# Expert products of a mixture-of-experts layer: split weights as moving operand, or unsplit 128x128 weight tiles as stationary operand

## The chip, the cores and the metric

One NeuronCore of a Trainium2 chip runs the whole program. The metric is the device time of one execution in microseconds (us). All data are float32.

## The reference, cut to what matters

One diffusion step of a one-layer hybrid model: 640 tokens (512 latent, 128 context) of 1024 features pass an mLSTM and an S5 branch and then an expert-choice mixture of experts. The change touches that last part alone:

```python
def ec_moe(h, w_router, b_router, w1, w3, w2):          # 16 experts, D 1024, FF 1536
    aff = jax.nn.softmax((h @ w_router) + b_router, axis=-1)
    topv, topi = lax.top_k(jnp.swapaxes(aff, 1, 2), cap) # 64 of 512 latents, 16 of 128 context tokens
    xe = h[topi]                                         # 80 rows of 1024 for each expert
    hid = silu(xe @ w1[e]) * (xe @ w3[e])                # 80 x 1536
    ye = (hid @ w2[e]) * topv                            # 80 x 1024
    return zeros.at[topi].add(ye)                        # scatter-add over tokens
```

Each expert reads three matrices of 1024x1536 float32, 18.9 MB; all sixteen read 302 MB.

## The kernel before, in words

The program is a row of blocks, each with a program for SP (which issues the weight loads), POOL (GpSimd, which issues gathers and scatters), PE (TensorE), ACT (ScalarE) and DVE (VectorE). First come the modulation, the S5 branch and the mLSTM heads; then the gates and projections (matmuls of L1309); then the router (from L1412), which turns the normalised tokens to rows, writes them to DRAM (`h2`) and picks 80 tokens for each expert; then the experts (from L1497); then a last block that reads the summed rows back and applies the final norm (from L1790).

Ahead of the expert block `load_piece` (L1242 to L1246) loads the first pieces: six while the last projections run, three more once the `h2` rows are written.

The expert block before. Each expert's hidden width of 1536 is cut into FG = 6 groups of 256. A piece is 1 MB: the 1024x256 columns of `w1` or `w3`, or 256 rows of `w2`, in a ring of three places for each name. Each piece is split for a product in three parts: ACT writes the high part `p_h` in the fp32r format (`high`, L1704), DVE writes `p_l`, the weight less that (`low`, L1749). The gathered tokens are turned by PE (`begin`, L1631) and split in the same way (L1698, L1741). In `up` (L1673) the 128x80 token tile is the stationary operand and 256 weight columns move, three matmuls for each of the 8 feature tiles: high by high, high by low, low by high. ACT applies silu (L1712), DVE multiplies (L1767), PE turns the hidden rows (`turn`, L1656), ACT and DVE split them (L1717, L1771), and `down` (L1646) multiplies them with `w2`, 512 columns moving. `take_y` (L1758, L1759) scales the 80x1024 result by the gate value; POOL clears a flag (L1608) and adds the rows into DRAM with an indirect DMA (L1610). Gathers (L1599) run two experts ahead. The order of PE in a step is up w1, turn, up w3, down of the step before. Loops (`Fori`) run over pairs of experts. SP waits for `w1_split`, `w3_split` and `w2_split`, which DVE raises when it has split a piece, before it loads into its place.

Other lines that the prediction reads: L676 multiplies 128x128 float32 stationary tiles by 80 float32 columns (S5 additions); L196 does it by 2 columns, L989 by 128 columns; L668 and L1441 are PE transposes of 128x128.

Of the kernel before, what the change touches and what calls it, by code (L numbers as in the profile page):

```python
# [20 lines left out]
P = 128  # L21
# [18 lines left out]
FG = 6  # L40
NRAW = 3
FT = FF // P // FG
# [29 lines left out]
def program(nc, ar, out):  # L72
    with ExitStack() as ctx:
# [1168 lines left out]
        PLACE = {"w1": (2, 7, 4), "w3": (3, 8, 0), "w2": (6, 5, 1)}  # L1242
        def load_piece(sp, name, e, q):
            sp.dma_start(place[:, PLACE[name][q % NRAW]],
                         ar["w_e" + name[1]][bass.ds(e, 1), q].rearrange("e p n -> p (e n)")
                         ).then_inc(sem(f"{name}_in{q % NRAW}"), 16)  # L1246

        with ExitStack() as st:
# [29 lines left out]
            @block.sync  # L1279
            def _(sp):  # L1280
                sp.dma_start(wr[:].rearrange("p k e -> p (k e)"), ar["w_router"]).then_inc(sem("wr_in"), 16)
                load_weights(sp, len(plan))

                sp.wait_ge(sem("parts_ready"), ends["B3"])
                load_piece(sp, "w1", 0, 0)
                load_piece(sp, "w3", 0, 0)
                load_piece(sp, "w2", 0, 0)
                load_piece(sp, "w1", 0, 1)
                load_piece(sp, "w3", 0, 1)
                sp.wait_ge(sem("parts_ready"), ends["O0"])  # L1290
                load_piece(sp, "w2", 0, 1)
# [110 lines left out]
        gidx = sb("gidx", [CAP, E], I32, moe)  # L1402
        with ExitStack() as st:  # L1403
# [9 lines left out]
            def token_rows(t):  # L1413

                return place[:, (0, 0, 1, 1, 4)[t], (t % 2) * D:(t % 2 + 1) * D]

            @block.sync
            def _(sp):
                sp.wait_ge(sem("h2_out"), 16 * NT)
                load_piece(sp, "w1", 0, 2)  # L1420
                load_piece(sp, "w3", 0, 2)
                load_piece(sp, "w2", 0, 2)
# [75 lines left out]
        with ExitStack() as st:  # L1498
# [4 lines left out]
            HC, HF = FT * CAP, FT * P  # L1503
            sl, hid = (rows[0:CAP, (4 + x) * D - x * D // 2:(4 + x) * D - x * D // 2 + D // 2].rearrange("p (b n) -> p b n", b=2)
                       for x in range(2))

            flag = sb("flag", [1, 1], F32, st)  # L1510
            x_h = sb("x_h", [P, 2, KD, CAP], F32R, st)
            x_l = sb("x_l", [P, 2, KD, CAP], F32R, st)
            hid_h = sb("hid_h", [P, 2, HC], F32R, st)
            hid_l = sb("hid_l", [P, 2, HC], F32R, st)
            PR = 4
            p_h = sb("p_h", [P, PR, KD * HF], F32R, st)
            p_l = sb("p_l", [P, PR, KD * HF], F32R, st)

            def parts(o, q, name):

                r = (3 * (o + q) + {"w1": 0, "w3": 1, "w2": 5}[name]) % PR
                return p_h[:, r, :], p_l[:, r, :]

            def up_tiles(ap):
                return ap.rearrange("p (k f) -> p k f", k=KD)

            def down_tiles(ap):
                return ap.rearrange("p (t d) -> p t d", t=FT)

            def raw(q, name):  # L1530
                return place[:, PLACE[name][q % NRAW], :]

            block = st.enter_context(nc.Block())

            def known(i, o, q, least):

                return not isinstance(i, int) or 2 * FG * i + o + q >= least

            def landed_at(i, o, q):

                return 16 * (2 * FG // NRAW) * i + 16 * ((o + q) // NRAW + 1)

            def experts(eng, begin, step, after=0):

                def half(i, o, h, coming=None):
                    for x, q in enumerate(range(h * FG // 2, (h + 1) * FG // 2)):
                        if coming and x == after:  # L1550
                            begin(*coming)
                        step(i, o, q)

                if after:
                    step(0, 0, 0)
                begin(0, 0)
                for q in range(1 if after else 0, FG // 2):
                    step(0, 0, q)
                half(0, 0, 1, (0, 1))
                half(0, FG, 0)  # L1560
                with eng.Fori(1, E // 2) as i:
                    half(i, -FG, 1, (i, 0))
                    half(i, 0, 0)
                    half(i, 0, 1, (i, 1))
                    half(i, FG, 0)
                half(E // 2 - 1, FG, 1)

            @block.sync
            def _(sp):
                def pieces(e, q):  # L1570

                    sp.wait_ge(sem("w1_split"), FG * e + (q - NRAW + 1))
                    load_piece(sp, "w1", e, q)
                    sp.wait_ge(sem("w3_split"), FG * e + (q - NRAW + 1))
                    load_piece(sp, "w3", e, q)
                    sp.wait_ge(sem("w2_split"), FG * e + (q - NRAW))
                    if q:
                        load_piece(sp, "w2", e, q - 1)
                    else:
                        load_piece(sp, "w2", e - 1, FG - 1)  # L1580

                sp.wait_ge(sem("w1_split"), 1)
                load_piece(sp, "w1", 0, 3)
                sp.wait_ge(sem("w3_split"), 1)
                load_piece(sp, "w3", 0, 3)
                for q in (4, 5):
                    pieces(0, q)
                with sp.Fori(1, E) as e:
                    for q in range(FG):
                        pieces(e, q)  # L1590
                sp.wait_ge(sem("w2_split"), FG * E - NRAW)
                load_piece(sp, "w2", E - 1, FG - 1)

            @block.gpsimd
            def _(pool):
# [7 lines left out]
                def scatter(e):  # L1603
# [11 lines left out]
                gather(0)  # L1615
                gather(1)
                for e in range(E):
                    if e + 2 < E:
                        gather(e + 2)
                    scatter(e)  # L1620
# [3 lines left out]
            PARTS = ((0, 0), (0, 1), (1, 0))  # L1624

            @block.tensor
            def _(pe):
                def begin(i, u):
                    pe.wait_ge(sem(f"xe_in{u}"), 16 * i + 16)
                    for k in range(KD):  # L1630
                        mm = pe.transpose(PS[4 + k // 4][:, (k % 4) * CAP:(k % 4 + 1) * CAP],  # L1631
                                          xe[:, u, k * P:(k + 1) * P], ident[0:CAP, 0:CAP])
                    mm.then_inc(sem("x_turned"), 1)

                def down(i, o, q):

                    n = 2 * FG * i + (o + q)
                    if q == 0 and known(i, o, q, FG):
                        pe.wait_ge(sem("y_ready"), 2 * i + o // FG)
                    pe.wait_ge(sem("hid_split"), n + 1)  # L1640
                    pe.wait_ge(sem("w2_split"), n + 1)
                    w2p = [down_tiles(x) for x in parts(o, q, "w2")]
                    for t in range(FT):
                        for x in range(2):
                            for j, (a, b) in enumerate(PARTS):
                                mm = pe.matmul(PS[2 + x][0:CAP, :], (hid_h, hid_l)[a][:, q % 2, t * CAP:(t + 1) * CAP],  # L1646
                                               w2p[b][:, t, x * 512:(x + 1) * 512],
                                               start=(q == 0 and t == 0 and j == 0),
                                               stop=(q == FG - 1 and t == FT - 1 and j == 2))
                    mm.then_inc(sem("down_done"), 1)  # L1650

                def turn(i, o, q):

                    pe.wait_ge(sem("hid_ready"), 2 * FG * i + (o + q + 1))
                    for t in range(FT):
                        mm = pe.transpose(PS[6 + q % 2][:, t * CAP:(t + 1) * CAP], hid[:, q % 2, t * P:(t + 1) * P],  # L1656
                                          ident[0:CAP, 0:CAP])
                    mm.then_inc(sem("hid_turned"), 1)

                def step(i, o, q):  # L1660
                    n = 2 * FG * i + (o + q)
                    u = (o // FG) % 2
                    if q == 0:
                        pe.wait_ge(sem("x_split"), 2 * i + (o // FG + 1))
                    if known(i, o, q, 2):
                        pe.wait_ge(sem("hid_ready"), n - 1)
# [13 lines left out]
                    elif known(i, o, q, 1):  # L1680
                        turn(i, o - FG, FG - 1)
# [241 lines left out]
```

## Time and profile before

| what | us |
|---|---|
| median of three runs (2022.3 to 2042.13) | 2038.01 |
| the profiled execution, its own time | 2040.35 |
| its span in the trace | 2038.3 |

### The profile page before, as it was taken

How to read it: one execution, taken by the hardware profiler on the slowest of the kernel's cores; microseconds unless marked ns; L12 is line 12 of the kernel's file. 1: busy time of each engine (PE TensorE's matmuls, PEld its weight loads, DVE VectorE, ACT ScalarE, POOL GpSimd, SP SyncE). 2: the span in 40 equal slices, each digit the busy share in tenths (PEclk: the TensorE clock that was granted, in tenths of full speed). 3: DMA queues.
4: the chain of work that ended last, by engine and by line, in shares of the span. 5: the costliest groups of instructions: out<-in, count | busy, mean ns of one | idle time of the engine just before them, and what ended most of it. 6: DMA issues, size and time to landing. Idle time of an engine off the chain costs nothing. (4 is left out here: it accounts for less than half of the span.)

```text
span 2038.3 us, 26524 instructions
## 1 busy us (share of the span) xinstructions
PE 1787.2 (88%) x10568; PEld 1407.4 (69%) x10568; DVE 1241.2 (61%) x1689; ACT 940.3 (46%) x1207; POOL 132.8 (7%) x92
## 2 busy tenths in 40 slices
PE   4775557999898986999997499999999999999993
PEld 2464444555464645999995488888888888888882
DVE  4577761013131314555554788888888888888874
ACT  3342222021212122444434377766666777766651
POOL 2600000000000000000000011100000011111000
PEclk8887768999898977999998699999999999999996
DMA  9032324102020110111230799999999999999953
GB/s 379 27 119 94 93 93 155 41 0 93 11 93 11 60 75 12 73 52 53 83 124 3 253 348 387 376 379 379 371 378 377 376 377 374 378 374 377 365 187 109
DMA packets 66698, 403.15 MB, mean 198 GB/s; under 512 B 12084, under 2 KB 18740, under 8 KB 25284
## 3 DMA queue, kind: packets, MB, share of 16 engines
q1 hardware_dynamic: 61476, 384.36, 49.7%
q0 software_dynamic: 5152, 17.84, 3.1%
q8 instruction: 47, 0.77, 0.2%
q14 instruction: 23, 0.19, 0.0%
HBM read 383.47 MB, written 16.56 MB: 196 GB/s over the span
## 5 line engine op out<-in xcount | busy, mean ns | idle before, releaser
L1749 DVE TENSOR_TENSOR p_l<-place,p_h 128x2048 fp32r<-128x2048 f32 x288 | 650.4, 2286 | 97.8 <-ACT p_h L1704 97.8
L1704 ACT ACTIVATE p_h<-place 128x2048 fp32r<-128x2048 f32 x288 | 540.3, 1911 | 26.3 <-PEq L1403 20.9
L1673 PE MATMUL bank<-p_h,x_h 128*80 128x256 f32 x1536 | 434.0, 283 | 1.8 <-DVE x_l L1741 1.8
L1673 PE MATMUL bank<-p_l,x_h 128*80 128x256 f32 x1536 | 429.6, 280 | 0.0
L1673 PE MATMUL bank<-p_h,x_l 128*80 128x256 f32 x1536 | 428.1, 279 | 0.0
L1673 PEld LDWEIGHTS bank<-p_h,x_h 128*80 128x80 f32 x1536 | 227.8, 148 | 9.4 <-DVE x_l L1741 2.0
L1673 PEld LDWEIGHTS bank<-p_l,x_h 128*80 128x80 f32 x1536 | 228.0, 148 | 6.1
L1673 PEld LDWEIGHTS bank<-p_h,x_l 128*80 128x80 f32 x1536 | 227.9, 148 | 0.0
L1309 PE MATMUL bank<-a_h,w_h 128*128 128x320 f32 x576 | 183.7, 319 | 19.6 <-DVE w_l L1390 10.9
L1309 PE MATMUL bank<-a_l,w_h 128*128 128x320 f32 x576 | 180.8, 314 | 0.0
L1309 PE MATMUL bank<-a_h,w_l 128*128 128x320 f32 x576 | 180.5, 313 | 0.0
L1646 PE MATMUL bank<-p_h,hid_h 128*80 128x512 f32 x384 | 150.6, 392 | 1.9 <-DVE hid_l L1771 1.9
L1646 PE MATMUL bank<-p_h,hid_l 128*80 128x512 f32 x384 | 151.8, 395 | 0.0
L1646 PE MATMUL bank<-p_l,hid_h 128*80 128x512 f32 x384 | 150.3, 391 | 0.0
L1717 ACT ACTIVATE hid_h<-bank 128x160 fp32r<-128x160 f32 x96 | 29.2, 304 | 241.1 <-PE bank L1656 241.1
L1000 PE MATMUL bank<-place,hT 128*128 128x512 f32 x320 | 138.0, 592 | 0.0
L1309 PEld LDWEIGHTS bank<-a_h,w_h 128*128 128x128 f32 x576 | 110.4, 192 | 26.3 <-DVE w_l L1390 12.7
L985 PE MATMUL bank<-hT,place 128*128 128x512 f32 x256 | 110.6, 592 | 2.2 <-PEq L866 2.2
L1000 PEld LDWEIGHTS bank<-place,hT 128*128 128x128 f32 x320 | 60.7, 190 | 74.8 <-issue 74.6
L1309 PEld LDWEIGHTS bank<-a_l,w_h 128*128 128x128 f32 x576 | 110.8, 192 | 0.0
L1309 PEld LDWEIGHTS bank<-a_h,w_l 128*128 128x128 f32 x576 | 110.7, 192 | 0.0
L1204 DVE TENSOR_TENSOR nd<-bank,rsb 128x257 f32<-128x257 f32 x32 | 13.6, 426 | 126.9 <-ACT rsb L1143 126.5
(353 smaller groups left out, 2304.2 us busy)
## 6 DMA issues: line engine op xcount, KB each, us to landing
place<-w_e_dram SPq DMA_DIRECT2D x288, 1024.0 KB, 7.6
place<-w_ada_dram SPq DMA_DIRECT2D x12, 2048.0 KB, 7.8
place<-w_qk_dram SPq DMA_DIRECT2D x4, 2048.0 KB, 9.2
place<-w_vo_dram SPq DMA_DIRECT2D x4, 2048.0 KB, 11.2
place<-w_gate_dram SPq DMA_DIRECT2D x4, 2048.0 KB, 7.4
place<-w_pAB_dram SPq DMA_DIRECT2D x4, 1536.0 KB, 6.4
place<-w_out_dram SPq DMA_DIRECT2D x2, 2048.0 KB, 7.3
xT<-xT_dram SPq DMA_DIRECT2D x1, 2560.0 KB, 17.7
```

The costliest lines, as they stand in the source:

```text
L985: mm = pe.matmul(PS[u % 2][:, :], w, hT[:, k, 0:LAT], start=(k == 0), stop=(k == 7))
L1000: mm = pe.matmul(PS[u % 2][:, :], hT[:, k, t * P:(t + 1) * P], wslot(c)[:, k, :], start=(k == 0), stop=(k == 7))
L1204: dve.tensor_tensor(nd[:, d, :], PS[3 + d][:, 0:DH + 1], Qs[:, d, :], ALU.add).then_inc(sem("nd_ready"), 1)
L1309: mm = pe.matmul(PS[bank][:, 0:TH], wp[:, n % RING, j * P:(j + 1) * P], ap[:, n % RING, x * TH:(x + 1) * TH], start=(k == 0 and i == 0), s ...
L1646: mm = pe.matmul(PS[2 + x][0:CAP, :], (hid_h, hid_l)[a][:, q % 2, t * CAP:(t + 1) * CAP], w2p[b][:, t, x * 512:(x + 1) * 512], start=(q == ...
L1673: mm = pe.matmul(PS[q % 2][0:CAP, at:at + HF], (x_h, x_l)[a][:, u, k, :], wp[b][:, k, :], start=(k == 0 and j == 0), stop=(k == 7 and j == 2))
L1704: act.activation(parts(o, q, name)[0], raw(q, name), ACT.Copy).then_inc(sem(f"{name}_high"), 1)
L1717: act.activation(hid_h[:, q % 2, :], PS[6 + q % 2][:, 0:HC], ACT.Copy).then_inc(sem("hid_high"), 1)
L1749: dve.tensor_tensor(l, raw(q, name), h.bitcast(F32), ALU.subtract).then_inc(sem(f"{name}_split"), 1)
```

## The change

- The weights of the experts are no longer split. In `up` a 128x128 tile of `w1` or `w3` is the stationary operand and the 80 tokens of `x` (features on partitions) move; the output is the hidden layer with its features on partitions, 12 tiles of 80 columns in two PSUM banks for each matrix. `down` uses 128x128 tiles of `w2` as stationary operand and `hid` moves. All of these are plain float32.
- Output y comes out turned; ACT copies it to SBUF (`take_y`), PE turns it back (`turn_y`, eight 128x80 tiles for each expert), DVE scales it (`leave_y`), POOL adds it to DRAM. The turning of the hidden rows, the splits of tokens and hidden values and the flag go.
- The pieces are 1.5 MB each, 4 for each matrix, 12 for each expert, 192 in all, in one ring of ten slots: five in the old place, five in a new tile `ring_tail`. PE raises `piece_used` after the last matmul on a piece, and SP waits for that. Five pieces are loaded while the projections end, three at the start of the router block, two once the `h2` rows are written. The token rows of the router stand in the last two slots of the new ring.
- Gathers are issued three experts ahead. The loops over experts are unrolled.
- PE's order for expert e: the four pieces of w1 (after the first `turn_y(e-2)`, after the third `turn_x(e+1)`), the four of w3, then `down(e-1)`.

The core of the diff:

```diff
-FG = 6
-FT = FF // P // FG
+NF = FF // P
+NR, PIECE, AHEAD_MOE = 10, 3072, 10
...
+        def load_piece(sp, n):
+            name, e, c = moe_pieces[n]
+            sp.dma_start(ring(n), ar["w_e" + name[1]][e, c]).then_inc(sem(f"piece_in{n % NR}"), 16)
...
-                    pool.memset(flag[:], 0.0).then_inc(sem("ys_free"), 1)
-                    pool.wait_ge(sem("ys_free"), e + 1)
...
+                for n in range(AHEAD_MOE, len(moe_pieces)):
+                    sp.wait_ge(sem("piece_used"), n - NR + 1)
+                    load_piece(sp, n)
...
-                        for k in range(KD):
-                            for j, (a, b) in enumerate(PARTS):
-                                mm = pe.matmul(PS[q % 2][0:CAP, at:at + HF], (x_h, x_l)[a][:, u, k, :], wp[b][:, k, :],
-                                               start=(k == 0 and j == 0), stop=(k == 7 and j == 2))
...
+                def turn_y(e):
+
+                    pe.wait_ge(sem("yT_ready"), e + 1)
+                    if e:
+                        pe.wait_ge(sem("y_ready"), e)
+                    for d in range(KD):
+                        mm = pe.transpose(PS[6 + d // 4][0:CAP, (d % 4) * P:(d % 4 + 1) * P], yT[:, d, :], ident)
+                    mm.then_inc(sem("y_turned"), 1)
+
+                def up(name, e, bank):
+                    for c in range(4):
+                        n = piece_at[name, e, c]
+                        have_piece(n)
+                        w = ring(n)[:, 0:2 * FF].rearrange("p (k f) -> p k f", k=2)
+                        for k in range(2):
+                            for f in range(NF):
+                                mm = pe.matmul(PS[bank + f // 6][:, (f % 6) * CAP:(f % 6 + 1) * CAP],
+                                               w[:, k, f * P:(f + 1) * P], x[:, e % 2, 2 * c + k, :],
+                                               start=(c == 0 and k == 0 and f % 6 == 0), stop=(c == 3 and k == 1),
+                                               skip_group_check=True)
+                        mm.then_inc(sem("piece_used"), 1)
+                        if name == "w1" and c == 0 and e >= 2:
+                            turn_y(e - 2)
+                        if name == "w1" and c == 2 and e + 1 < E:
+                            turn_x(e + 1)
...
+                        w = ring(n)[:, 0:3 * D].rearrange("p (t d) -> p t d", t=3)
+                        for t in range(3):
+                            for d in range(KD):
+                                mm = pe.matmul(PS[4 + d // 4][:, (d % 4) * CAP:(d % 4 + 1) * CAP],
+                                               w[:, t, d * P:(d + 1) * P], hid[:, e % 2, 3 * c + t, :],
+                                               start=(c == 0 and t == 0 and d % 4 == 0), stop=(c == 3 and t == 2),
+                                               skip_group_check=True)
...
+                for e in range(E):
+                    pe.wait_ge(sem("x_ready"), e + 1)
+                    if e:
+                        pe.wait_ge(sem("silu_ready"), e)
+                    up("w1", e, 0)
+                    if e:
+                        pe.wait_ge(sem("hid_ready"), e)
+                    up("w3", e, 2)
+                    if e:
+                        down(e - 1)
+                down(E - 1)
+                turn_y(E - 1)
...
-                    act.activation(parts(o, q, name)[0], raw(q, name), ACT.Copy).then_inc(sem(f"{name}_high"), 1)
...
-                    dve.tensor_tensor(l, raw(q, name), h.bitcast(F32), ALU.subtract).then_inc(sem(f"{name}_split"), 1)
```

## Rows read from the trace of the kernel before

**Rows 1.** The page: DMA busy tenths and GB/s in 40 equal slices.

```profile
DMA  9032324102020110111230799999999999999953
GB/s 379 27 119 94 93 93 155 41 0 93 11 93 11 60 75 12 73 52 53 83 124 3 253 348 387 376 379 379 371 378 377 376 377 374 378 374 377 365 187 109
```

**Rows 2.** Stretches: PE, PEld, DVE, ACT, POOL busy (x records), PEclk, DMA share, GB/s.

```profile
1149.50:1157.00 7.50, 5.65 (x28) 5.41 (x29) 5.02 (x4) 2.56 (x3) 0.94 (x1) 0.50 0.87 294
...
1160.00:1950.00 790.00, 789.12 (x5784) 694.65 (x5783) 697.10 (x518) 557.77 (x488) 77.49 (x43) 1.00 0.99 373
```

**Rows 3.** SP's DMA queue waiting between 1200 and 1900 us: us, times, longest.

```profile
SPq L1244 <- DVE p_l L1749: 577.7, 242, 4.4
```

**Rows 4.** PE's timeline in the expert block: x transposes, fp32r matmuls 21 starts apart.

```profile
1149.57 1.33 PE L1631 MATMUL bank<-consts,hT 80*128 80x80 f32 x8 [5.31 <-DMA hT<-h_dram,gidx]
...
1281.26 0.72 PE L1631 MATMUL bank<-consts,hT 80*128 80x80 f32 x8
...
1973.68 0.28 PE L1673 MATMUL bank<-p_h,x_h 128*80 128x256 f32 x1
...
1976.13 0.28 PE L1673 MATMUL bank<-p_h,x_h 128*80 128x256 f32 x1
```

**Rows 5.** Timeline of the end of the expert block, and the end of its last loads.

```profile
1930.08 30.81 SPq L1244 DMA_DIRECT2D place<-w_e_dram  x10
...
1988.12 0.74 DVE L1759 TENSOR_SCALAR hT<-bank,gval 80x512 f32<-80x512 f32 x1
...
1989.29 1.42 POOL L1610 DMA_INDIRECT moe_dram<-hT,gidx  x1 [0.28 <-POOL flag L1608]
```

**Rows 6.** PE's timeline: start us, us, stationary (128*128, 128*16), then moving operand, records.

```profile
565.80 7.31 PE L989 MATMUL bank<-hT,place 128*128 128x128 f32 x64
...
119.02 7.16 PE L697 MATMUL bank<-CA,bbz 128*16 128x128 f32 x64
...
242.38 3.70 PE L676 MATMUL bank<-U,place 128*128 128x80 f32 x32
...
248.65 1.05 PE L196 MATMUL bank<-sel,adar 128*128 128x2 f32 x8 [0.72 <-ACT adar L202]
```

**Rows 7.** Durations of single records of these lines (ns, min/median/max).

```profile
L989 PE MATMUL bank<-hT,place x256: 272/275/276, 372.6 to 685.6; 128*128 128x128 f32 x128
...
L676 PE MATMUL bank<-U,place x128: 235/275/422, 114.8 to 245.8; 128*128 128x80 f32 x128
...
L196 PE MATMUL bank<-sel,adar x96: 251/251/374, 14.4 to 310.6; 128*128 128x2 f32 x96
```

**Rows 8.** Timeline of PE in the router (128x128 transposes), then of SP, POOL and ACT.

```profile
1117.15 1.97 PE L1441 MATMUL bank<-consts,hT 128*128 128x128 f32 x16
...
1129.12 27.06 SPq L1244 DMA_DIRECT2D place<-w_e_dram  x6
...
1145.53 0.97 POOL L1599 DMA_INDIRECT hT<-h_dram,gidx  x1 [20.80 <-POOLq L1403]
...
1150.94 0.77 ACT L1698 ACTIVATE x_h<-bank 128x320 fp32r<-128x320 f32 x2 [2.40 <-PE bank L1631]
```

**Rows 9.** The costliest groups of ACT and DVE: busy us, mean ns, idle before.

```profile
L1749 DVE TENSOR_TENSOR p_l<-place,p_h 128x2048 fp32r<-128x2048 f32 x288 | 650.4, 2286 | 97.8 <-ACT p_h L1704 97.8
L1704 ACT ACTIVATE p_h<-place 128x2048 fp32r<-128x2048 f32 x288 | 540.3, 1911 | 26.3 <-PEq L1403 20.9
```

**Rows 10.** Two stretches of L676, and the unrolled projections (columns of rows 2).

```profile
137.90:139.90 2.00, 2.00 (x11) 2.00 (x11) 1.97 (x3) 0.60 (x1) 0.00 (x0) 0.50 0.04 8
139.90:142.40 2.50, 2.50 (x24) 2.49 (x23) 2.43 (x3) 0.00 (x0) 0.00 (x0) 1.00 0.00 0
...
242.40:246.00 3.60, 3.60 (x34) 3.53 (x32) 3.53 (x4) 0.63 (x2) 0.00 (x0) 1.00 0.00 0
...
870.00:1090.00 220.00, 210.20 (x1368) 203.85 (x1367) 116.78 (x205) 92.77 (x172) 0.00 (x0) 0.98 0.19 72
```

**Rows 11.** DMA of instructions between 870 and 1090 us: packets, MB, share.

```profile
q8 instruction: 11, 0.18, 0.3%
```

More of the change, by code:

```diff
@@ L1284, in _ @@
                 sp.wait_ge(sem("parts_ready"), ends["B3"])
[L1285 to L1289, printed above, removed]
+                for n in range(3):
+                    load_piece(sp, n)
                 sp.wait_ge(sem("parts_ready"), ends["O0"])
-                load_piece(sp, "w2", 0, 1)
+                load_piece(sp, 3)
+                sp.wait_ge(sem("parts_ready"), ends["O1"])
+                load_piece(sp, 4)
             @block.tensor
@@ L1530, in raw @@
-            def raw(q, name):
-                return place[:, PLACE[name][q % NRAW], :]
-            block = st.enter_context(nc.Block())
[L1537 to L1566, printed above, removed]
+            x = sb("x", [P, 2, KD, CAP], F32, st)
@@ L1582, in _ @@
[L1582 to L1592, printed above, removed]
+                for n in range(AHEAD_MOE, len(moe_pieces)):
+                    sp.wait_ge(sem("piece_used"), n - NR + 1)
+                    load_piece(sp, n)
@@ L1613, in scatter @@
                                             ).then_inc(sem(f"y_out{e % 2}"), 16)
-                gather(0)
-                gather(1)
+                for e in range(3):
+                    gather(e)
                 for e in range(E):
-                    if e + 2 < E:
-                        gather(e + 2)
+                    if e + 3 < E:
+                        gather(e + 3)
                     scatter(e)
@@ L1630, in begin @@
                     for k in range(KD):
-                        mm = pe.transpose(PS[4 + k // 4][:, (k % 4) * CAP:(k % 4 + 1) * CAP],
-                                          xe[:, u, k * P:(k + 1) * P], ident[0:CAP, 0:CAP])
+                        mm = pe.transpose(PS[6 + k // 4][:, (k % 4) * CAP:(k % 4 + 1) * CAP],
+                                          xe[:, e % 2, k * P:(k + 1) * P], ident[0:CAP, 0:CAP])
                     mm.then_inc(sem("x_turned"), 1)
[L1635 to L1644, printed above, removed]
-                            for j, (a, b) in enumerate(PARTS):
[L1646 to L1650, printed above, removed]
@@ new lines, in down @@
+                def down(e):
+                    pe.wait_ge(sem("hid_ready"), e + 1)
+                    if e:
+                        pe.wait_ge(sem("yT_ready"), e)
+                    for c in range(4):
+                        n = piece_at["w2", e, c]
+                        have_piece(n)
+                        w = ring(n)[:, 0:3 * D].rearrange("p (t d) -> p t d", t=3)
[5 more added lines that the diff above has]
+                                               skip_group_check=True)
+                        mm.then_inc(sem("piece_used"), 1)
+                        if e == E - 1 and c == 0:
+                            turn_y(e - 1)
@@ L1732, in _, with take_x @@
-                experts(act, begin, step, after=1)
-                finish(E // 2 - 1, FG, FG - 1)
+                def take_x(e):
+                    act.wait_ge(sem("x_turned"), e + 1)
+                    if e >= 2:
+                        act.wait_ge(sem("piece_used"), piece_at["w3", e - 2, 3] + 1)
+                    for y in range(2):
+                        ins = act.activation(x[:, e % 2, 4 * y:4 * y + 4, :].rearrange("p k c -> p (k c)"),
+                                             PS[6 + y][:, 0:4 * CAP], ACT.Copy)
+                    ins.then_inc(sem("x_ready"), 1)
@@ new lines, in take_y @@
+                def take_y(e):
+                    act.wait_ge(sem("piece_used"), piece_at["w2", e, 3] + 1)
+                    if e:
+                        act.wait_ge(sem("y_turned"), e)
+                    for y in range(2):
+                        ins = act.activation(yT[:, 4 * y:4 * y + 4, :].rearrange("p k c -> p (k c)"),
+                                             PS[4 + y][:, 0:4 * CAP], ACT.Copy)
+                    ins.then_inc(sem("yT_ready"), 1)
+                take_x(0)
+                for e in range(E):
+                    if e + 1 < E:
+                        take_x(e + 1)
+                    act.wait_ge(sem("piece_used"), piece_at["w1", e, 3] + 1)
+                    if e:
+                        act.wait_ge(sem("hid_ready"), e)
+                    for h in range(2):
+                        ins = act.activation(sl[:, h, :], PS[h][:, 0:6 * CAP], ACT.Silu)
+                    ins.then_inc(sem("silu_ready"), 1)
+                    if e:
+                        take_y(e - 1)
@@ new lines, in _ @@
+                for e in range(E):
+                    if e >= 2:
+                        leave_y(e - 2)
+                    dve.wait_ge(sem("silu_ready"), e + 1)
+                    dve.wait_ge(sem("piece_used"), piece_at["w3", e, 3] + 1)
+                    if e >= 2:
+                        dve.wait_ge(sem("piece_used"), piece_at["w2", e - 2, 3] + 1)
+                    for h in range(2):
+                        ins = dve.tensor_tensor(hid[:, e % 2, 6 * h:6 * h + 6, :].rearrange("p f c -> p (f c)"),
+                                                sl[:, h, :], PS[2 + h][:, 0:6 * CAP], ALU.mult)
+                    ins.then_inc(sem("hid_ready"), 1)
```

193 lines of the change are left out of this document (46 added, 147 removed).

## The prediction

> **What bounds the kernel now.** I read the page first, for the stages. Its 40 slices are 51 us each. From slice 24 to 38 the DMA row stands at 9 and the GB/s row between 348 and 387: these are the experts. Between the first slice and slice 21 no more than 155 GB/s are moved [rows 1]. The reader should see that nothing ahead of about 1100 us is touched by the change, so it is the expert block that has to be priced. I read next the stretches of that block. From 1160 to 1950 us PE is busy 789.12 of 790 us and the 16 DMA engines have a share of 0.99 at 373 GB/s, both at once, at full clock [rows 2]. Then SP's waits: its queue stands 577.7 us, in 242 waits, for DVE to have split a piece [rows 3], so loads start when a place is free, and places come free at the pace of the split chain.
>
> So two limits lie almost on each other. The weights: 16 x 3 x 1024 x 1536 x 4 bytes are 302 MB, and 302 MB at the 377 GB/s of the best slices takes 801 us. The matmuls: an fp32r matmul of 256 columns follows the one before at 2.45 us / 21 = 117 ns [rows 4], and PE does 3 x 16 x 96 = 4608 of these, and 1152 of 512 columns; their end is near 1987 us, only some 26 us after the last load's landing at 1960.9 us [rows 5]. A change gains only if it relieves both; it loses as soon as either one grows. This one leaves the bytes as they are.
>
> **The change, part by part.**
>
> *Products of the experts.* Each expert needs 8 x 12 tiles for w1, as many for w3, and 12 x 8 for w2: 288 products of a 128x128 stationary tile with 80 moving columns, 4608 in all. A plain float32 product is two LDWEIGHTS and two MATMULs, so 9216 pairs of records. What does one pair cost? The trace of before has exactly this shape at L676. Its fourth stretch lies at full clock and takes 3.70 us for 32 records: (3.70 - 0.235) / 31 = 111.8 ns from start to start (a record at full clock lasts 0.235 us [rows 7]). L989 has the same stationary tile and 128 moving columns: (7.31 - 0.275) / 63 = 111.7 ns. L196 has it with 2 moving columns: (1.05 - 0.251) / 7 = 114 ns [rows 6, 7]. Two, eighty or 128 moving columns cost the same. What sets the pace is therefore the load of the 128 stationary columns and not what streams, and the 80 tokens' short stream buys nothing. I take 111.7 ns: 9216 x 0.1117 = 1029.4 us. The nearest rows bound it: L697 loads only 16 stationary columns for 128 moving ones, (7.16 - 0.27) / 63 = 109.4 ns, a record's 0.27 us as in L989 [rows 6], which I take as the low end for any pair of this kind that doesn't hide its load; and 117 ns if the expert block with its full DMA traffic slowed it to the fp32r pace [rows 4]. That is 1008 to 1078 us.
>
> [...]
>
> *Transposes.* Tokens: 8 for each expert, as before, (0.72 - 0.235) / 7 = 69 ns apart at full clock [rows 4], a record's 0.235 us as at L676: 128 x 0.070 = 8.9 us. Output: 8 for each expert are new, 128 moving columns each; L1441 does 16 in 1.97 us, (1.97 - 0.27) / 15 = 113 ns [rows 8], 128 x 0.113 = 14.5 us. The 192 transposes of hidden rows go. PE's whole work is then 1029.4 + 8.9 + 14.5 = 1052.8 us, 65.8 us for each expert, where before an expert took 52 us, (1987 - 1152.7) / 16.
>
> *What goes from ACT and DVE.* The 288 high parts and 288 low parts, 540 and 650 us of busy time [rows 9]. They lie beside PE and DMA. Their going is worth nothing by itself once PE is the bound: DVE keeps two scalings and two products for each expert, ACT a handful of copies.
>
> *The ring.* A piece of 1.573 MB lasts PE 24 products x 2 x 0.1117 = 5.36 us, and DMA at 377 GB/s 4.17 us. Ten pieces are ahead at the start and SP refills faster than PE uses, so PE never waits for a piece, and the DMA share falls to about 302 MB / 1055 us = 286 GB/s, some 77%. So I cost the loading at nothing; PE's work on the pieces hides it, and were that cover gone, DMA's 801 us would still be the smaller of the two limits.
>
> *Waits on PE.* `turn_y(e-2)` needs two ACT copies of 128x320 (0.43 us each by [rows 8]: 0.77 us for two); it stands behind one piece, 5.4 us. `turn_x(e+1)` needs the two scalings of DVE (0.74 us each [rows 5]); it stands two pieces, 10.7 us, behind `turn_y`. silu and the product for expert e are needed only after four pieces of w2, 21 us. The gather of expert e+3 is queued on POOL ahead of the scatter of expert e, waits for `turn_x(e+1)`, and has more than one expert, 65 us, until it is used. What stands behind these waits on PE is everything, so a miss would count in full, but the shortest cover is seven times what it covers. I cost them at nothing, with 0 to 1 us for each expert (0 to 16 us) kept for the range.
>
> *Start.* The first gather is issued at 1145.53 us and PE turns the tokens from 1149.57 us [rows 4, 8]. The two extra pieces are issued once `h2` is written, at 1129.12 us before [rows 8], and 3.1 MB take 8 us, so the gather finds the queues free as before. ACT's copies end at 1151.7 us; the low part's split of tokens falls out, and the first product starts at 1151.8 instead of 1152.7 us. PEclk is 0.50, the level of 1.2 GHz, until 1157 us, and 1.00 from 1160 us on [rows 2]; 5.3 us at half rate lose 2.7 us.
>
> *End.* After the last product: two copies of ACT and two hops 1.1 us, then the transposes (counted), then two scalings 1.5 us. Before, L1759 ends at 1988.86 us and from there to the end of the span are 49.4 us; the scatter's issue is at 1989.29 us, 0.43 us behind it [rows 5], and without the flag I save 0.3 us of these.
>
> **Sum.** 1151.8 + 1052.8 + 2.7 + 1.1 + 1.6 = 2210.0; + 49.4 - 0.3 = 2259.1 us of span. The profiled execution took 2.05 us more than its span and lies 2.3 us above the median of the runs, so the two cancel: 2259 us, a change of +221 us, 11% slower.
>
> **The rivals.**
>
> *A, faster: the load hides and the weights' transfer is the bound.* Place: the spacing of the 9216 pairs. If loads of the next tile ran wholly beside the stream of 80 columns, a pair would cost what the stream takes; from 5.36 us a piece it decides from the point where a piece costs PE less than 4.17 us, or a pair less than 87 ns. Then the 182 pieces not loaded ahead take 759 us from about 1157 us on, the last is used and turned by about 1924 us, and the end is at 1975 us. For it speaks that the moving operand is now only 80 columns and that the split work of two engines is gone. Against it speak three lines of rows 6 with 2, 80 and 128 columns at one pace. Chance 6%. [...]
>
> *B, the clock stays or falls to 1.2 GHz.* PE streams fewer columns in a given time than before. At half clock pairs are some 214 ns apart, twice as far as at full clock: in L676's second stretch 2.0 us at 0.50 hold 11 records, the next 2.5 us at 1.00 hold 24 [rows 10]; a block wholly at this level costs 2 x 1052.8 us, and the end is near 3310 us. Against it: the same L676 pace was under way at 137.9 us at 0.50 and the clock rose to 1.00 during it, and at 242.4 us it was at 1.00 all through [rows 10]. Those stretches are short. Chance 4%.
>
> *C, the unrolled program starves PE of instructions.* Between 870 and 1090 us, also unrolled, 2735 records of PE came with 11 packets of instructions [rows 10, 11], one for some 250. The new block has 18,900 PE records, so about 76 packets, and DMA is at 77% share and not at 19% as there. If PE stood 2 us for each packet (an estimate: half of the 4.0 us from the first gather's issue to PE's start [rows 4, 8]), it is 152 us more: 2411 us. Against it: PE is busy 210 of 220 us in that unrolled stage. Chance 6%; a part of it, 20 to 40 us, is more likely than the whole.
>
> *D, the pipeline of small waits costs over 16 us*, for instance because PE stands for the two copies, the two scalings and the hops between, some 3 us [rows 5, 8], once for each expert: 16 x 3 us = 48 us, 2307 us. Chance 3%.
>
> **How the numbers follow.** The forecast 81%, A 6%, B 4%, C 6%, D 3%. The range from the bounds: low 2259 - 21 = 2238, and 6 us less for the start, 2232; high 2259 + 49 (117 ns) and a few us of waits, 2315, which takes in D. Left out are A, B and the dear half of C. A measurement of this kernel tells about 1% from no change: faster by over 1% is A, 6%; within 1% 1%; slower 93%.
>
> **What would show it.** L1673's successors should stand 111 to 112 ns apart in the timeline at PEclk 1.00, 24 x 2 in 5.4 us, PE busy over 99% from 1160 to 2200 us, PEld nearer to PE than before; the DMA share of that stretch near 0.77 and under 300 GB/s; SP's queue waiting for PE (`piece_used`) most of its time; DVE and ACT busy under 10% there. PE waiting for a DMA, or PE starts under 90 ns apart, would make the forecast wrong at its root (A); PEclk under 1.00 would be B; idle time of PE put down to issue would be C.

## The result and the profile after

The changed kernel takes 2360.03 us (median of four runs, 2349.64 to 2363.95) against 2039.74 us: ratio 1.158, 95% interval 1.151 to 1.166, slower. The sign was forecast, the size was not: 2259 us had been given, with a range up to 2315. The span of its profiled execution is 2358.7 us. An execution of any of these programs takes one of two courses through the mLSTM stage, and PE begins to turn the first expert's tokens at 1147 to 1152 us in the late one and at 1132 to 1137 us in the early one; the profiled executions of the kernels before and after took the late one.

The page of the changed kernel, with the rows that answer to [rows 1] and the one of PE's granted clock:

```profile
span 2358.7 us, 30959 instructions
...
PE   4965579989898699998599999999999999999993
...
DVE  4577720122121455564300000000000000000003
ACT  3333210222212244444000000000000000000001
POOL 1500000000000000000000000000000000000000
PEclk7877789989898799999555589999999999999997
DMA  8222330020202012121543478888888888888822
GB/s 327 76 86 85 103 152 36 1 90 1 89 13 104 11 63 90 72 108 65 211 165 139 157 260 301 301 298 296 298 296 303 295 297 300 303 295 292 297 85 94
...
q8 instruction: 109, 1.79, 0.3%
```

A slice is now 59 us. PE is full from slice 21 on, ACT and DVE are all but empty, and the DMA row stands at 8 where it stood at 9: PE alone is the bound, as forecast. But look at the clock: slices 20 to 23 stand at 5 and slice 24 at 8, and in all of them but the first, in which the block starts, PE is full. The stretches on either side of the rise (columns as in [rows 2]), and SP's queue between 1200 and 2250 us:

```profile
1150.00:1369.00 219.00, 219.00 (x1034) 218.84 (x1035) 2.44 (x5) 5.64 (x11) 1.00 (x2) 0.50 0.41 148
1369.20:2200.00 830.80, 830.80 (x7488) 830.80 (x7488) 33.88 (x52) 32.56 (x76) 29.76 (x25) 1.00 0.84 298
```

```profile
SPq L1260 <- PE bank L1590: 691.3, 121, 11.0
SPq L1260 <- PE bank L1610: 300.4, 56, 9.9
```

PE has not one idle microsecond in either stretch; it does 4.7 records each us in the first and 9.0 in the second. SP waits for PE 992 of 1050 us, where [rows 3] had it wait for DVE. And the timeline of PE: the start of the block, a piece of work under the lower clock, the place of the rise, and 144 records under the full clock:

```profile
1147.60 1.33 PE L1570 MATMUL bank<-consts,hT 80*128 80x80 f32 x8 [5.46 <-DMA hT<-h_dram,gidx]
1149.79 30.58 PE L1590 MATMUL bank<-x,place 128*128 128x80 f32 x142 [0.85 <-ACT x L1639]
...
1315.84 41.17 PE L1610 MATMUL bank<-hid,ring_tail 128*128 128x80 f32 x192
1356.80 10.45 PE L1590 MATMUL bank<-x,place 128*128 128x80 f32 x48
1367.04 1.92 PE L1580 MATMUL bank<-consts,yT_e 128*80 128x128 f32 x8
...
2222.27 1.04 PE L1580 MATMUL bank<-consts,yT_e 128*80 128x128 f32 x8
2223.14 16.20 PE L1590 MATMUL bank<-x,ring_tail 128*128 128x80 f32 x144
```

Under the full clock a pair costs (16.20 - 0.24) / 143 = 111.6 ns: the forecast's number to a tenth. Under the lower one it is (41.17 - 0.42) / 191 = 213.4 ns. The clock rises 2 us after the first `turn_y` begins at 1367.04 us. 219 us at 213.4 in place of 111.6 ns lose 219 x (1 - 111.6 / 213.4) = 104.5 us; the forecast had 2.7. With the block's start 2.0 us earlier than I had it, 2259.1 + 101.8 - 2.0 = 2358.9 us, against 2358.7 measured. So the miss lies in one term. What had to be found out was why the clock stayed low beside a busy PE, and whether it was the shape of the work.

### The profile page after: what moved, and what is told of

The parts are those of the page before. It is cut to its first block and busy times, and to the rows that moved or that the text cites. A ratio compares the mean times of both kernels' runs of the same rounds, so it can differ in the third digit from the quotient of the medians.

```text
span 2358.7 us, 30959 instructions
## 1 busy us (share of the span) xinstructions
PE 2107.6 (89%) x13960; PEld 1827.9 (77%) x13960; DVE 549.8 (23%) x1209; ACT 395.5 (17%) x791; POOL 88.7 (4%) x76
## 5 line engine op out<-in xcount | busy, mean ns | idle before, releaser
L1590 PE MATMUL bank<-x,place 128*128 128x80 f32 x3120 | 407.6, 300 | 0.9 <-ACT x L1639 0.9
L1590 PEld LDWEIGHTS bank<-x,place 128*128 128x128 f32 x3120 | 405.1, 216 | 1.1 <-ACT x L1639 1.1
L1590 PE MATMUL bank<-x,ring_tail 128*128 128x80 f32 x3024 | 371.3, 289 | 0.0
L1590 PEld LDWEIGHTS bank<-x,ring_tail 128*128 128x128 f32 x3024 | 369.3, 205 | 0.0
L1610 PE MATMUL bank<-hid,ring_tail 128*128 128x80 f32 x1536 | 193.4, 293 | 0.9 <-issue 0.9
L1610 PEld LDWEIGHTS bank<-hid,ring_tail 128*128 128x128 f32 x1536 | 192.2, 210 | 1.0 <-issue 1.0
L1610 PE MATMUL bank<-hid,place 128*128 128x80 f32 x1536 | 173.6, 275 | 0.0
L1610 PEld LDWEIGHTS bank<-hid,place 128*128 128x128 f32 x1536 | 172.6, 192 | 0.0
L1674 DVE TENSOR_SCALAR hT<-bank,gval 80x512 f32<-80x512 f32 x32 | 22.5, 742 | 438.9 <-PE bank L1580 438.9
L985 PEld LDWEIGHTS bank<-hT,place 128*128 128x128 f32 x256 | 48.3, 190 | 61.6 <-issue 61.6
```

The costliest lines, as they stand in the source:

```text
L985: mm = pe.matmul(PS[u % 2][:, :], w, hT[:, k, 0:LAT], start=(k == 0), stop=(k == 7))
L1590: mm = pe.matmul(PS[bank + f // 6][:, (f % 6) * CAP:(f % 6 + 1) * CAP], w[:, k, f * P:(f + 1) * P], x[:, e % 2, 2 * c + k, :], start=(c == ...
L1610: mm = pe.matmul(PS[4 + d // 4][:, (d % 4) * CAP:(d % 4 + 1) * CAP], w[:, t, d * P:(d + 1) * P], hid[:, e % 2, 3 * c + t, :], start=(c == ...
L1674: ins = dve.tensor_scalar(ys[:, e % 2, 512 * h:512 * h + 512], PS[6 + h][0:CAP, :], gval[:, e:e + 1], None, ALU.mult)
```

## The experiments

### e1: a burst of wide products first

```diff
                 turn_x(0)
+                for j in range(4):
+                    pe.matmul(PS[4][:, 0:512], ident, xT[:, j, 0:512], start=True, stop=True)
                 for e in range(E):
```

> The changed kernel with four float32 products of 512 moving columns (eight records, into a PSUM bank that nobody uses yet) between the first turning of the tokens and the first expert product. In the changed kernel PEclk stood at 0.50 until 1369.1 us although PE was busy all the time. Theory (activity): products with 80 moving columns behind a 128-column load do not bring the clock up, wide ones do, and once it is up the products hold it. Then it rises within the burst or just behind it, near 1155 us, stays at 1.00 to the end of the experts, and the span is 2358.7 - (1369 - 1155) / 2 + 6 for the burst = 2258 us, about 1.105 of before. Rival (a cap at the start): something of the first experts, for instance their dense loads or the end of the work of ACT and DVE, holds the clock down until about 1369 us whatever PE does; then no gain, 2365 us. Second rival (the clock cannot be held): it rises in the burst and falls again in the first expert, 2355 us.

Measured: 2260.91 us (four runs, 2260.66 to 2261.31), ratio 1.1125 (1.1055 to 1.1196), span 2258.8, late course. PE's timeline and then stretches of e1, columns as before:

```profile
1148.43 6.37 PE L1620 MATMUL bank<-xT,consts 128*128 128x512 f32 x8
1154.63 15.53 PE L1590 MATMUL bank<-x,place 128*128 128x80 f32 x138
```

```profile
1148.50:1153.80 5.30, 5.30 (x9) 2.20 (x8) 0.00 (x0) 0.77 (x2) 0.90 (x1) 0.50 0.23 62
1154.00:1200.00 46.00, 46.00 (x412) 45.56 (x411) 1.22 (x2) 3.08 (x5) 0.90 (x1) 1.00 0.71 251
1200.00:2200.00 1000.00, 999.10 (x8998) 998.98 (x8998) 39.35 (x60) 37.69 (x88) 32.59 (x27) 1.00 0.80 285
```

PEclk is still 0.50 up to 1153.8 us and 1.00 from 1154.0 us on, 5.6 us after the eight wide records began, whose results are thrown away, and it stays there for the whole block. 6 us of useless work save 100 us. There is no cap at the start; the products do hold a clock that they had not raised in 217 us. The forecast's sum without its clock term and with this start gives 2259.1 - 2.7 + (1154.6 - 1151.8) = 2259.2 us, against 2258.8 measured, so the other terms stand.

### e2 and e7: eight or sixteen transposes of turn_y's shape

```diff
+                        if name == "w1" and c == 0 and e == 0:
+                            for d in range(KD):                      # e7: sixteen
+                                pe.transpose(PS[6 + d // 4][0:CAP, (d % 4) * P:(d % 4 + 1) * P], ident[:, 0:CAP], ident)
                         if name == "w1" and c == 2 and e + 1 < E:
```

> The changed kernel with eight transposes of the shape of turn_y (128x80 stationary, 128 moving columns) behind the first piece of the first expert, where the changed kernel has none. In the changed kernel the clock rose at 1369.1 us, 2 us after the first turn_y began. Theory: that run of eight with 128 moving columns is what raised it; then it rises here near 1164 us, and the span is 2358.7 - (1369 - 1164) / 2 + 1 = 2257 us. Rival (the place in time was chance, or another cause of the start): it rises where it did, 2360 us.

> e2 with sixteen transposes of 128 moving columns in place of eight behind the first piece of the first expert. In e2 eight at this place did not bring the clock up, while the first turn_y did, 200 us later. Theory (a run of wide moves raises it, and eight are just on the edge, so that it depends on how they fall): sixteen raise it at once, at about 1166 us, span 2358.7 - (1369 - 1166) x 0.48 + 3 = 2264 us. Rival (float32 products are needed, transposes do not count, and the rise at the first turn_y was chance): it rises where it did, 2363 us.

e2 took 2363.5 us (one run, span 2361.4), as the rival said; e7 took 2263.7 us (one run, span 2261.8), as the theory said; both in the late course. PE's timeline of e2, the eight and later the first `turn_y`; then its stretches:

```profile
1161.23 1.91 PE L1599 MATMUL bank<-consts 128*80 128x128 f32 x8
1162.93 17.41 PE L1590 MATMUL bank<-x,place 128*128 128x80 f32 x81
...
1369.79 1.92 PE L1580 MATMUL bank<-consts,yT_e 128*80 128x128 f32 x8
```

```profile
1163.00:1373.00 210.00, 210.00 (x993) 209.84 (x993) 3.70 (x6) 5.64 (x11) 0.90 (x1) 0.50 0.42 154
1374.00:2200.00 826.00, 826.00 (x7445) 826.00 (x7445) 32.10 (x50) 32.56 (x76) 29.18 (x25) 1.00 0.83 297
```

The same in e7:

```profile
1159.67 3.62 PE L1599 MATMUL bank<-consts 128*80 128x128 f32 x16
```

```profile
1150.00:1163.90 13.90, 13.90 (x68) 13.55 (x67) 0.00 (x0) 0.00 (x0) 0.00 (x0) 0.50 0.30 100
1164.10:1200.00 35.90, 35.90 (x327) 35.90 (x326) 0.00 (x0) 3.08 (x5) 0.90 (x1) 1.00 0.73 266
```

Eight such transposes at 1161 us leave the clock at 0.50; eight at 1367 or 1370 us are followed by 1.00, 2 us and nearly 4 us after they begin; sixteen at 1160 us are followed by 1.00 within 1 us of their end. So a run of transposes with 128 moving columns can raise the clock. Whether eight of them did depended on the place; why was not tried further.

### e3 and e4: without the runs of turn_y

```diff
-                    for d in range(KD):
+                    for d in (KD - 1,):                              # in turn_y; e4 has the burst of e1 as well
```

> The changed kernel with one instead of eight transposes in each turn_y (seven eighths of the turned output are left out). Theory: nothing of 128 dense moving columns is left in the expert block, so the clock stays at 1.2 GHz to its end: 2 x (1029 + 9) us of products and token transposes from 1149 us on, a span of about 3280 us. Rival (the clock rises by itself after some 200 us): near 1370 us as before, and 14 us less of transposes, 2347 us.

> The burst of e1 and the single output transpose of e3 together (the same part of the output left out). It tells whether the products hold the clock by themselves once it is up, or whether turn_y has to raise it again for every expert. Theory (holds by itself): 1.00 from about 1155 us to the end, span 2258 - 12 = 2246 us. Rival (needs turn_y): it falls within one or two experts and stays down, up to 3270 us.

e3 took 3173.15 us (one run, span 3171.4), e4 2231.3 us (one run, span 2229.5), both in the early course (first product at 1134.5 us in e3). A long stretch of each:

```profile
1400.00:3000.00 1600.00, 1600.00 (x7543) 1600.00 (x7542) 34.12 (x52) 32.55 (x76) 28.78 (x24) 0.50 0.45 158
```

```profile
1137.00:2100.00 963.00, 963.00 (x8669) 962.37 (x8668) 37.95 (x58) 38.96 (x89) 32.10 (x27) 1.00 0.84 298
```

These two differ only in eight records of burst and lie 942 us apart. In e3 PE is busy 1600 of 1600 us and the clock never rises. In e4 the same products keep it up without the runs of `turn_y`. So the products hold either level they meet. e3 came out about 100 us under its expectation: I had doubled 111.7 ns where 213.4 is measured (9216 x 0.010 = 92 us), and the early course gave 15 us. e4 in the late course would have a span of about 2245 us; 2246 had been expected.

### e6 and e10: fewer tokens, with the burst

```diff
...
-                                               w[:, k, f * P:(f + 1) * P], x[:, e % 2, 2 * c + k, :],
+                                               w[:, k, f * P:(f + 1) * P], x[:, e % 2, 2 * c + k, 0:40],   # e10: 0:64
...
```

(the same for `hid`, and outputs as wide as the operand; e1's burst ahead)

> e1 with only 40 of the 80 tokens moving (half of the output left out). The load theory says that a pair takes as long as with 80, 111 to 112 ns while the clock is at 2.4 GHz. What moves in a given time is halved, so this run also asks how near the edge the clock is: if the products of 80 columns hold it with room, the span is that of e1, 2259 us; if the level follows what moves, it falls in the first expert and the pairs go to some 213 ns, about 3200 us.

> e1 with 64 of the 80 tokens moving (a fifth of the output left out). With 80 the clock held at 2.4 GHz for 1050 us, with 40 it fell 7 us after the burst. The pair costs 112 ns in both cases by the load theory. If the edge of holding lies under 64 columns: 2259 us as in e1; if 80 is just above it: it falls in the first expert, some 3200 us.

e6 took 3210.49 us, e10 2255.45 us (one run each; e6 in the late course, e10 in the early one and with a burst 1.6 us shorter). PE's timelines of e6 and of e10, each followed by its stretches:

```profile
1154.64 25.21 PE L1590 MATMUL bank<-x,place 128*128 128x40 f32 x144
...
1201.17 51.40 PE L1590 MATMUL bank<-x,ring_tail 128*128 128x40 f32 x240
```

```profile
1154.00:1160.60 6.60, 6.60 (x57) 6.15 (x55) 0.00 (x0) 0.00 (x0) 0.00 (x0) 1.00 0.00 0
1161.00:1200.00 39.00, 39.00 (x188) 39.00 (x187) 0.00 (x0) 3.08 (x5) 0.90 (x1) 0.50 0.47 171
```

```profile
1142.18 16.19 PE L1590 MATMUL bank<-x,place 128*128 128x64 f32 x144
```

```profile
1200.00:2100.00 900.00, 900.00 (x8115) 900.00 (x8113) 35.33 (x54) 35.11 (x82) 29.80 (x25) 1.00 0.83 298
```

With 64 columns the pair costs (16.19 - 0.22) / 143 = 111.7 ns, as with 80 and 128 (and 114 with 2 [rows 6]). With 40 columns the clock, up after the burst, was at 0.50 again from 1161 us and stayed there, with (51.40 - 0.38) / 239 = 213.5 ns a pair. Fewer tokens save nothing, neither 64 at 1.00 nor 40 at 0.50, and with 40 of them the clock was lost. With 64 it was lost once, near the end of e10, where PE stood for 0.90 us, as it does there in the changed kernel and in e1 too:

```profile
2170.55 10.40 PE L1610 MATMUL bank<-hid,ring_tail 128*128 128x64 f32 x48 [0.90 <-issue]
```

```profile
2171.00:2184.00 13.00, 13.00 (x63) 12.84 (x63) 1.31 (x2) 0.00 (x0) 0.00 (x0) 0.50 0.01 1
```

The clock was down from there for 14 us, until past the next transposes of 128 columns, and the 48 records took 10.40 us instead of 5.5. With 80 columns the changed kernel and e1 pass that place at 1.00.

### e5 and e11: half the stationary columns

```diff
...
-                                               w[:, k, f * P:(f + 1) * P], x[:, e % 2, 2 * c + k, :],
+                                               w[:, k, f * P:f * P + 64], x[:, e % 2, 2 * c + k, :],
...
```

(the same in `down`, outputs on 64 partitions; e11 also loads each piece with two DMAs of half rows)

> The changed kernel with only the first 64 of the 128 columns of each stationary tile loaded; the same number of products, half of each one's output left out, the loads from DRAM unchanged. Theory (the load of the stationary columns sets the pace of a pair): the distance falls from 112 ns to what 80 moving columns need, some 70 ns, PE needs 9216 x 0.070 = 645 us, and the weights' transfer becomes the bound: the expert block ends some 780 us after its start, a span near 1975 us, DMA share 0.99. The pace of moving columns is denser, so the clock comes up in the first expert. Rival (a fixed price for each pair, not the load): 112 ns stay, 2360 us.

> e5 (bound by the weights' transfer at 409 GB/s, where the kernel before moved 377 with rows of 8 KB) with each piece loaded by two DMAs of 6 KB rows instead of one of 12 KB rows. If the length of a row is what raised the rate: under 377 GB/s, the block takes at least 800 us, span over 1985 us (or 1965 if the early stages take their shorter time). Rival (row length is not it, the kernel before was held by its waits for places): 409 GB/s again, 1927 to 1945 us.

e5 took 1929.24 us (one run, span 1927.5, early course), e11 1949.88 us (one run, span 1948.1, late course). PE's timeline of e5, four of its stretches, and one of e11:

```profile
1155.17 16.76 PE L1590 MATMUL bank<-x,ring_tail 128*64 128x80 f32 x240
```

```profile
1138.00:1140.00 2.00, 2.00 (x19) 2.00 (x17) 0.00 (x0) 0.00 (x0) 0.00 (x0) 0.53 0.08 16
1140.00:1142.00 2.00, 2.00 (x32) 2.00 (x30) 0.00 (x0) 0.00 (x0) 0.00 (x0) 1.00 0.00 0
1200.00:1500.00 300.00, 282.23 (x3895) 273.96 (x3893) 17.15 (x26) 17.95 (x42) 16.55 (x14) 1.00 1.01 409
1500.00:1800.00 300.00, 276.12 (x3730) 264.94 (x3728) 16.95 (x26) 15.38 (x36) 13.21 (x11) 0.99 1.01 413
```

```profile
1200.00:1700.00 500.00, 468.72 (x6371) 455.63 (x6369) 28.86 (x44) 26.39 (x62) 26.00 (x22) 0.98 1.02 408
```

With 64 stationary columns the same number of pairs with the same 80 moving columns stand (16.76 - 0.24) / 239 = 69 ns apart. Nothing else was changed on PE, so the load of the stationary tile set the 111.7 ns: this is the direct test of the forecast's main step, and it is also rival A built by hand. The DMA engines are then the bound, but at 409 to 413 GB/s and not at the 377 I had taken for their limit by the best slices of [rows 1]. Rows of 6 KB in e11 move 408 GB/s where rows of 12 KB in e5 move 409, so the length of a row isn't the reason.

The first two stretches bear on the clock. e5 has no burst and no early transposes; its first product starts at 1135.6 us with PEclk at 0.50, and from 1140 us on it is 1.00. So the same 80 moving columns did raise the clock behind a load of 64 columns, which they did not in 1600 us behind one of 128 (e3).

### e8: the operands swapped

```diff
-                            for f in range(NF):
-                                mm = pe.matmul(PS[bank + f // 6][:, (f % 6) * CAP:(f % 6 + 1) * CAP],
-                                               w[:, k, f * P:(f + 1) * P], x[:, e % 2, 2 * c + k, :],
+                            for f in range(3):
+                                mm = pe.matmul(PS[bank + f % 2][0:CAP, :],
+                                               x[:, e % 2, 2 * c + k, :], w[:, k, f * 512:(f + 1) * 512],
...
```

(`down` in the same way)

> The changed kernel with the operands swapped: the 80 tokens (or the hidden values) are the stationary tile and 512 unsplit weight columns move, plain float32, same ring, same transposes and copies (the sums land where the rest does not expect them, so the output is not the layer's). 72 products for each expert, 144 records. Theory: each takes the 429 ns of other 512-column records of this program, the clock rises in the first expert, PE needs 16 x (61.8 + 1.5) = 1013 us, span about 2219 us: 40 us under e1, and 180 us over the kernel before. Rival (DMA-bound or hindered by the transfers): above 2240 us.

Measured: 2202.91 us (one run, span 2201.1, early course, so a span of some 2216 in the late one). PE's timeline:

```profile
1511.44 20.77 PE L1590 MATMUL bank<-place,x 128*80 128x512 f32 x48
```

(20.77 - 0.59) / 47 = 429 ns for a record that covers four tiles of 128 columns: 2 x 429 / 4 = 215 ns for the work that the changed kernel does in 2 x 111.6 = 223. Unsplit float32 costs nearly the same in either arrangement; this one brings its clock up by itself, from 0.50 up to 1138 us to 1.00 from 1140 us on, with its first product at 1135.3 us. At 0.50 its records start 853 ns apart (the second at 1136.22 us and the third after it at 1138.78 us), twice the 429 ns at 1.00.

### e9: the kernel before with bfloat16 halves

```diff
-            p_h = sb("p_h", [P, PR, KD * HF], F32R, st)
+            p_h = sb("p_h", [P, PR, KD * HF], BF16, st)
```

(the same for `p_l`, `x_h`, `x_l`, `hid_h`, `hid_l`, and without the bitcasts)

> [...] If a bfloat16 record costs its columns and 3 ns, PE needs 4608 x 0.110 + 1152 x 0.216 + 24 = 780 us instead of 834, and the transfer's 801 us become the bound: the block ends some 30 us earlier, ratio 0.985. Rival: the split chain of ACT and DVE or SP's waits set the end of the block and not PE: ratio 1.00.

Measured: 1993.65 us (six runs, 1979.77 to 2003.03), ratio to the kernel before 0.978 (0.973 to 0.983), where 0.985 had been expected. A stretch of e9, and starts on PE, the first two 12 records of 512 columns apart, the last two 16 of 256:

```profile
1160.00:1900.00 740.00, 731.22 (x5708) 618.00 (x5707) 682.47 (x508) 548.76 (x482) 73.95 (x41) 1.00 1.01 392
```

```profile
1455.24 0.38 PE L1647 MATMUL bank<-p_h,hid_h 128*80 128x512 bf16 x1
...
1457.83 0.27 PE L1674 MATMUL bank<-p_h,x_h 128*80 128x256 bf16 x1
...
1499.93 0.27 PE L1674 MATMUL bank<-p_h,x_h 128*80 128x256 bf16 x1
...
1501.68 0.27 PE L1674 MATMUL bank<-p_l,x_h 128*80 128x256 bf16 x1
```

1.75 us / 16 = 109 ns for what took 117 in fp32r [rows 4], and (1457.83 - 1455.24) / 12 = 216 ns for 512 columns. In the kernel before twelve fp32r records of 512 columns start at 1451.95 us, and the next record of 256 at 1454.72 us:

```profile
1451.95 0.40 PE L1646 MATMUL bank<-p_h,hid_h 128*80 128x512 f32 x1
...
1454.72 0.28 PE L1673 MATMUL bank<-p_h,x_h 128*80 128x256 f32 x1
```

(1454.72 - 1451.95) / 12 = 231 ns. The 110 and 216 ns of the expected sum were the author's estimate, which no run before e9 shows; e9 has 109 and 216. 256 more columns take 216 - 109 = 107 ns there at PEclk 1.00, 2.4 columns a nanosecond, the number that the legend of PEclk sets beside 1.00.

PE now has idle time, 9 of 740 us, and the transfer runs at 392 GB/s where it ran at 373 [rows 2], with the share of the DMA engines at 1.01 and 0.99. The split chain did not become faster: a piece takes ACT 1904 ns and DVE 2286 ns, as against 1911 and 2286 [rows 9]. It is the fastest kernel of this study that computes the layer, and its split parts are in bfloat16.

## Why the prediction was right in its sign and wrong in its size

**The products: right.** 111.7 ns was taken from L676 and L989; measured 111.6 over the block, unmoved by 298 GB/s of transfers. e5 (69 ns with 64 stationary columns) and e10 (111.7 with 64 moving ones) show that the load is the cause.

**The transposes: right.** `turn_y` costs (1.04 - 0.27) / 7 = 110 ns each, 113 were taken.

**Waits, ring and start: right.** After its first product PE stands still inside the block only twice, 0.9 us each: once for ACT's copy of the last expert's result, and once ahead of the last `down`, where the trace names no releaser; the DMA share is 0.84 and the rate 298 GB/s at full clock, where I had 0.77 and 286 as a mean over the block; the first product starts at 1149.8 us, forecast 1151.8. Rival C has nothing for it: 109 packets of instructions instead of 47, and PE idle for none. (The sum adds 1.6 us for the two scalings that its working puts at 1.5; 0.1 us changes nothing.)

**The clock: this is the step that failed.** In "Start" I let PEclk rise at 1157 us because it did so in the kernel before [rows 2]. But there the first products moved 256 columns behind an 80-column load. The new ones move 80 behind a 128-column load. I had seen that question as rival B and gave it 4%, and only its extreme, a block wholly at PEclk 0.50; a block at 0.50 for its first 219 us, which is what came, stood neither in the sum nor in the range nor in a rival. The clock term of 2.7 us measured 104.5 us. Against B I had set L676, which was under way at 0.50 when the clock rose, and at 1.00 all through later [rows 10]. The first half of that argument was wrong: it took the products as the reason for the rise without asking what PE had done just ahead of them. In the same execution, PE's timeline of the kernel before reads:

```profile
134.39 3.68 PE L668 MATMUL bank<-consts,place 128*128 128x128 f32 x16 [8.21 <-DVE place L478]
137.86 4.68 PE L676 MATMUL bank<-U,place 128*128 128x80 f32 x32
```

The 80-column records followed a run of sixteen 128-column transposes, which by e7 can raise the clock. That it was they that raised it there was not tested; 80-column records behind a load of 128 columns did not do it in e3. The second half, that they hold a raised clock, was right (e1, e4). So there are three cases, not two: work that raises the clock, work that holds what it finds, and work that lets it fall (e6). The price of B was off as well: B names 214 ns for a pair but then doubles the whole sum, and 213.4 ns is 1.91 times 111.6, not twice.

**Rival A's price: wrong.** It gave 1975 us with the transfer at 377 GB/s. e5 and e11 do that case in 1927 and 1948 us, since the same bytes move at 409. From the DMA share of 0.99 I had concluded that two limits lay on each other. e9 shows that PE was the nearer one: with a faster PE, unchanged loads and an unchanged split chain the rate rose from 373 to 392 GB/s. That its 373 GB/s were no limit can be seen in the kernel before itself, when the block from 1160 to 1950 us is cut into 40 slices of 20 us each:

```profile
GB/s 323 341 368 356 415 351 390 388 344 419 362 380 392 337 403 368 343 420 341 391 383 353 414 365 370 393 346 395 376 340 418 363 373 390 343 409 369 365 360 365
```

Single slices reach 420, so the 377 GB/s of the slices of 51 us [rows 1] was a mean over faster and slower stretches, and not the limit that I took it for. Why e5 gets 409 from its ring and e9 392 was not tried. What differs in the traces is how long a piece takes from issue to landing, 35.6 us in e5 and 7.5 us in e9 (medians between 1160 and 1900 us). At one piece of 1.573 MB in 3.85 us (409 GB/s) and one of 1.049 MB in 2.7 us (392 GB/s) that is an estimated nine pieces under way at once in e5 and three in e9.

## What to carry to other kernels

Count a float32 product by the larger of its two sides, the stationary columns loaded and the columns moved. A product is two records, and for each of them this case has 112 to 114 ns with 128 stationary columns and 2, 64, 80 or 128 moving ones, 69 ns with 64 stationary and 80 moving (e5), and 429 ns with 80 stationary and 512 moving (e8). When products become narrow, price the stage at both clock levels, and read in the trace what PE did ahead of a rise and not only during it; a few microseconds of wide throwaway products at the start of such a stage are worth a try (6 us bought 100 here). And a DMA share near 1 did not prove that the transfers were at their limit.

## What the runs showed of the hardware that I had not expected

- PE busy for 1600 of 1600 us at PEclk 0.50 (e3): a full PE row in the profile does not mean the full clock.
- The same stream of products ran for 963 us at 1.00 or 1600 us at 0.50, by what stood ahead of it (e4, e3); with 40 moving columns it lost 1.00 within 7 us (e6).
- 80 moving columns behind a load of 64 columns brought the clock from 0.50 to 1.00 within 5 us (e5); behind a load of 128 they did not in 1600 us (e3).
- The distance of load-bound pairs is 111.6 ns at 1.00 and 213.4 ns at 0.50.
- 256 moving columns take 117 ns in fp32r and 109 ns in bfloat16, 512 take 231 and 216.
- The DMA engines gave 373, 392 and 409 GB/s at a share of 0.99, 1.01 and 1.01.
